# Gates as seven products of half blocks, kept in DRAM until the branch products

## The reference

```
branches = einsum('btgc,gcd->btgd', stack([out_a, out_b, out_c]), w_branch)   # 3 x (512 -> 1024)
gates    = sigmoid(h @ w_gate + b_gate).reshape(b, t, 3, d)                   # 1024 -> 3 x 1024
x        = x + sum(gates * branches, axis=2) @ w_out
h2       = rms_norm(x, norm_ffn)
x        = x + (silu(h2 @ w_ffn_gate) * (h2 @ w_ffn_up)) @ w_ffn_down
```

## Time and profile before

| | us |
|---|---|
| median of 3 runs | 3132.02 |
| lowest and highest | 3129.63, 3132.77 |
| span of the profiled execution, first to last instruction | 3129.0 |

### The profile page before, as it was taken

One profiled execution on the slowest core, in us unless ns is written; L12 is line 12 of the kernel. 1 busy time (PEld: TensorE's weight loads), 2 busy tenths in 40 slices (PEclk: granted clock), 3 DMA queues, 4 the chain that ended last, 5 costly groups with the idle time before them and its releaser, 6 DMA issues.

```text
span 3129.0 us, 50323 instructions
## 1 busy us (share of the span) xinstructions
PE 3066.4 (98%) x18600; PEld 2608.8 (83%) x18600; DVE 1791.4 (57%) x3573; ACT 1329.6 (42%) x2637; POOL 664.3 (21%) x886
## 2 busy tenths in 40 slices
PE   7999999999999999999999999998999999999999
PEld 7988888999999888888788888888977777787777
DVE  6657674353344322345888887876353666753675
ACT  5446565454445221232333333454433555522552
POOL 3423334453542000001111111001101011032240
PEclk9999999999999999999999999999999999999999
DMA  5110011011111321122233225643100000221012
GB/s 204 37 48 18 21 35 51 28 62 44 56 59 46 103 78 51 45 95 97 72 109 109 102 101 204 196 151 140 46 28 22 16 28 15 108 72 67 28 61 101
DMA packets 77412, 231.27 MB, mean 74 GB/s; under 512 B 17712, under 2 KB 21936, under 8 KB 65648
## 3 DMA queue, kind: packets, MB, share of 16 engines
q1 hardware_dynamic: 77168, 228.05, 20.8%
HBM read 183.92 MB, written 43.84 MB: 73 GB/s over the span
## 4 chain that ended last, share of the span: by engine, by line
PE 90%; DVE 6%; ACT 2%; issue 1%; DMA 1%; SPq 0%; POOL 0%; DVEq 0%; ACTq 0%; POOLq 0%
PE ps L2546 71%; PE ps L2589 7%; PE ps L2597 3%; PE ps L2553 2%; PE ps L2604 2%; PE ps L2620 2%; PE ps L2612 1%; PE ps L2623 1%; PE ps L2640 1%; DVE wlo L2815 0%; DVE hlo L2892 0%; ACT hhi L2660 0%; ACT whi L2650 0%; DVE qk L2923 0%; DMA fa2r<-scratch_fs 0%
## 5 line engine op out<-in xcount | busy, mean ns | idle before, releaser
L2546 PE MATMUL ps<-whi,hhi 128*128 128x256 f32 (+2 forms) x1920 | 580.5, 302 | 3.0 <-DVE hlo L2892 1.7
L2546 PE MATMUL ps<-whi,hlo 128*128 128x256 f32 (+2 forms) x1920 | 563.7, 294 | 0.0
L2546 PE MATMUL ps<-wlo,hhi 128*128 128x256 f32 (+2 forms) x1920 | 563.4, 293 | 0.0
L2546 PEld LDWEIGHTS ps<-whi,hhi 128*128 128x128 f32 x1920 | 368.2, 192 | 12.8 <-issue 5.1
L2546 PEld LDWEIGHTS ps<-wlo,hhi 128*128 128x128 f32 x1920 | 368.8, 192 | 7.4 <-issue 0.2
L2546 PEld LDWEIGHTS ps<-whi,hlo 128*128 128x128 f32 x1920 | 368.2, 192 | 7.7
L2546 PE MATMUL ps<-hhi,whi 128*128 128x512 f32 x864 | 342.3, 396 | 0.0
L2546 PE MATMUL ps<-hhi,wlo 128*128 128x512 f32 x864 | 337.0, 390 | 0.0
L2546 PE MATMUL ps<-hlo,whi 128*128 128x512 f32 x864 | 336.3, 389 | 0.0
L3154 POOL TENSOR_SCALAR stats<-stats 128x2 f32<-128x2 f32 (+2 forms) x230 | 59.3, 258 | 1194.1 <-ACT xsf L2654 509.1
L3143 POOL CAST whi<-raw 128x512 fp32r<-128x512 f32 (+4 forms) x180 | 113.7, 631 | 865.8 <-PE ps L2546 856.1
(11 more groups left out here) (616 smaller groups left out, 6996.6 us busy)
## 6 DMA issues: line engine op xcount, KB each, us to landing
raw<-in_W SPq DMA_DIRECT2D x61, 1024.0 KB, 4.8
scratch_fs<-fo SPq DMA_DIRECT2D x77, 256.0 KB, 2.0
raw<-in_W SPq DMA_DIRECT2D x24, 768.0 KB, 4.3
wd<-in_WD SPq DMA_DIRECT2D x44, 256.0 KB, 3.5
wf0b<-in_WF SPq DMA_DIRECT2D x10, 1024.0 KB, 5.3
wf1b<-in_WF SPq DMA_DIRECT2D x10, 1024.0 KB, 5.2
scratch_x<-x SPq DMA_DIRECT2D x16, 512.0 KB, 3.3
orw<-scratch_outs SPq DMA_DIRECT2D x6, 1024.0 KB, 5.8
```

The lines of the kernel that those rows point to most:

```text
L2546: x = e.matmul(r.out, a, b, start=(r.start and m == 0), stop=(r.stop and m == n - 1), skip_group_check=r.joined)
```

## The change

The gates are computed first, for all branches, and stored in a DRAM scratch `gates`; the branch products come after them and read the gates back tile by tile. The 24 strips form 12 pairs (strip x with strip x + 12). The first pair is plain (`plain_gates`: four outputs of 24 matmuls, in eight blocks of 12). For each of the other eleven, the two strips by two halves of tokens and two halves of the 1024 features are a product of 2 by 2 half blocks, made of seven products of 4 k (84 matmuls) whose results are added by VectorE (`ff_add`). For this the token operands t1 to t4 are built from `hhi` and `hlo` (`combine`, `op_split`; t1 in place over the late tokens' first features), on VectorE, partly in attention's tail (`gate_front`), partly among pair 1. Two weight sets alternate. The sums of weights for pair 1 are made by VectorE, for pairs 2 to 11 by GpSimd. The weight stream is now released in three stages (`w_release`), w_branch comes in chunks of 256 columns, and the first and second branch's outputs are split into the space of `hhi` and `hlo`. `b_merge(3, 1)` moves from before the gates into pair 2. `WeightSet`, `combine`, `op_split`, `ff_add` and the product are moved up and shared with the feed-forward, which is otherwise unchanged.

```diff
+GATE_PAIRS = 12
+GATE_STRIPS = [8 * g + d for g in GATE_ORDER for d in range(8)]
...
+    add(("w_gate", 0, 8, [(128 * GATE_STRIPS[x], 128) for x in (0, GATE_PAIRS)]))
+    held = [len(plan)]
     for g in GATE_ORDER:
-        for d in range(8):
-            add(("w_gate", 0, 8, [(g * 1024 + d * 128, 128)]), ("w_branch", g * 512, 4, [(d * 128, 128)]))
+        for c in range(4):
+            add(("w_branch", g * 512, 4, [(256 * c, 256)]))
...
-        def w_release(*free):
-
-            w_held[0] = False
-            raw_free[:], spl_free[:] = [flat(*free), flat(*free)], [flat(*free), flat(*free)]
-            for _ in range(2):
+        def w_release(raws, slots, loads=2):
+            w_stage[0] += 1
+            raw_free[:], spl_free[:] = raws, slots
+            for _ in range(loads):
...
-                    for hf in range(2):
-                        r = Rec()
-                        r.cut = slice(hf * 512, hf * 512 + 512)
-                        r.gate = DB.take()
-                        mm3(r.gate, r.gate.ps[:, :], views(ch.part(0), slice(0, 128)), views(hpair, r.cut), 8, ch.split)
-                        r.si, r.t, r.t_free = scr.take()
-                        r.bias = hb_gate[:, g * 8 + dd:g * 8 + dd + 1]
-                        emit("gate_tanh", r)
-                        gm["gate"] = r.gate.full
-                        halves.append(r)
-                        yield
...
-                            r.branch = DB.take()
-                            gm["branch"] = mm3(r.branch, r.branch.ps[:, :], views(ch.part(1), slice(0, 128)),
-                                               views((ohi, olo), r.cut), 4, ch.split, osp)
-                            r.mix, r.first, r.mix_free = mix[:, dd_, r.cut], first, flat(b_free if dd_ > 3 else b_read) if first else []
-                            r.mixed = r.branch.read if first else signal("mix_added")
-                            emit("gate_mix", r)
...
+            def load(self, i, *free):
+                self.landed = load(self.landing, self.of(i).raw4[:, :, :], self.source[i], *free, self.done[:4])
+            def sums(self, i, *free, pool=False):
+                a11, a12, a21, a22, s1, s2, s4 = self.of(i).raw
+                sum1 = combine(pool, s1, a21, a22, ALU.add, self.landed, self.done[4], *free)
+                sum3 = combine(pool, a21, a11, a21, ALU.subtract)
+                sum2 = combine(pool, s2, s1, a11, ALU.subtract, self.done[5])
+                sum4 = combine(pool, s4, a12, s2, ALU.subtract, self.done[6])
+                self.ready = [self.landed, self.landed, sum3, self.landed, sum1, sum2, sum4]
...
+        g_ops = {
+            "b11": [(lambda k, w=w: w[:, k, early]) for w in hpair], "b21": [(lambda k, w=w: w[:, k + 4, early]) for w in hpair],
+            "b22": [(lambda k, w=w: w[:, k + 4, late]) for w in hpair], "t1": [(lambda k, w=w: w[:, k, late]) for w in (hlo, hhi)],
+            "t2": [(lambda k, w=w: w[:, k, :]) for w in (gt2h, gt2l)], "t3": [(lambda k, w=w: w[:, k, :]) for w in (gt3h, gt3l)],
+            "t4": [(lambda k, w=w: w[:, k, :]) for w in (gt4h, gt4l)],
+        }
...
+        gsets = [
+            WeightSet("wg0", d["WG"], of(0) * 2, of(16) * 2, [of(22, 24, 26, 28, 30, 8, 10)] * 2),
+            WeightSet("wg1", d["WG"], of_rest(80.5) * 2, of(32) * 2, [of(12, 38, 40, 42, 44, 14, 46)] * 2),
+        ]
...
+            gate_kept[x, hf] = store(f"fs{at_ + j}", d["gates"][x, :, 512 * hf:512 * hf + 512], outs[j], r.done)
...
+            def p1(self):
+                self.m1 = self.product(1, self.a.take())
+            def keep(self):
+                evac(self.m1, [(self.x, self.m1.ps[:, :])], gX_free[self.i % 2])
+            def p2(self):
+                self.c11 = self.product(2, self.a.take(), joined=True)
+            def out11(self):
+                gate_out(self.c11.ps[:, :], self.i, 0, self.c11.full, go, go_free, 0, self.c11)
+            def p6(self):
+                self.m6 = self.product(6, self.b.take())
+                ff_add(self.x, self.m6, self.x)
+            def p7(self):
+                self.m7 = self.product(7, self.c.take())
+            def u3(self):
+                ff_add(gU, self.m7, self.x, gU_free)
+            def p5(self):
+                self.m5 = self.product(5, self.d.take())
+            def out22(self):
+                c22 = ff_add(gU, self.m5, gU)
+                gU_free[:] = [gate_out(gU, self.i + GATE_PAIRS, 1, c22, go, go_free, 1)]
+            def p4(self):
+                self.m4 = self.product(4, self.c.take(), joined=True)
+            def out21(self):
+                c21 = ff_add(gV, self.m4, self.x, gV_free)
+                gV_free[:] = [gate_out(gV, self.i + GATE_PAIRS, 0, c21, go, go_free, 2)]
+            def p3(self):
+                self.m3 = self.product(3, self.d.take(), joined=True)
+            def out12(self):
+                c12 = ff_add(self.x, self.m3, self.x)
+                gX_free[self.i % 2] = [gate_out(self.x, self.i, 1, c12, go, go_free, 3)]
...
+        def gate_front():
+            s, b_last = gsets[1], b_vlast[0]
+            s.load(0, b_last, b_fin[2, 3], qk_n_free)
+            yield
+            next(gate_piece)
+            yield
+            gsets[0].load(1, b_last, spl_done[held[0] - 1])
+            yield
+            next(gate_piece)
+            s.sums(0, b_last)
+            yield
+            s.split(0, 0, free=b_last)
+            yield
+            for x, c in enumerate(g_two):
+                near = [b_units[55].v_full, b_units[55].s_full, b_units[55].exps]
+                combine(False, gt3[:, c, :], b_at(g_hi, 1, late, c), b_at(g_hi, 0, late, c), ALU.subtract, near)
+                combine(False, gt3[:, c, :], gt3[:, c, :], b_at(g_lo, 1, late, c), ALU.add)
+                yield
+                next(gate_piece)
+                three[x] = combine(False, gt3[:, c, :], gt3[:, c, :], b_at(g_lo, 0, late, c), ALU.subtract)
+                s.split(0, (2, 1)[x], free=b_last)
+                yield
+            s.split(0, 5, free=b_last)
+            yield
+            for x, c in enumerate(g_two):
+                two[x] = combine(False, gt2[:, c, :], gt3[:, c, :], b_at(g_hi, 0, early, c), ALU.add, b_units[63].s_full)
+            yield
+        gate_gen = gate_front()
...
+                next(gate_gen, None)
...
+        next(gate_piece)
+        s = GatePair(1)
+        near = [b_units[55].s_full, b_units[55].v_full]
+        for x, c in enumerate(g_two):
+            g_read["t3"].append(op_split(gt3[:, c, :], gt3h[:, c, :], gt3l[:, c, :], three[x], two[x], near))
+        for x, c in enumerate(g_two):
+            two[x] = combine(False, gt2[:, c, :], gt2[:, c, :], b_at(g_lo, 0, early, c), ALU.add)
+        four = [combine(False, gt4[:, c, :], b_at(g_hi, 1, early, c), gt2[:, c, :], ALU.subtract, b_read, gp_free) for c in g_two]
+        for x, c in enumerate(g_two):
+            g_read["t2"].append(op_split(gt2[:, c, :], gt2h[:, c, :], gt2l[:, c, :], two[x], four[x], b_read))
+        for _ in range(3):
+            next(gate_piece)
+        drain(gate_piece)
+        s.p1()
+        s.keep()
+        t1_free = [g_plain[0], g_plain[1]]
+        s.p7()
+        for c in g_two:
+            out = gt1[:, c, late]
+            combine(False, out, b_at(g_hi, 0, late, c), b_at(g_hi, 0, early, c), ALU.subtract, t1_free)
+            combine(False, out, out, b_at(g_lo, 0, late, c), ALU.add)
+            one = combine(False, out, out, b_at(g_lo, 0, early, c), ALU.subtract)
+            g_read["t1"].append(op_split(out, hlo[:, c, late], hhi[:, c, late], one, None, None))
+        s.p2()
+        s.out11()
+        s.p6()
+        s.u3()
+        gsets[1].split(0, 4, 3, free=b_vlast[0])
+        s.p5()
+        for x, c in enumerate(g_two):
+            four[x] = combine(False, gt4[:, c, :], gt4[:, c, :], b_at(g_lo, 1, early, c), ALU.add)
+            g_read["t4"].append(op_split(gt4[:, c, :], gt4h[:, c, :], gt4l[:, c, :], four[x], None, b_read))
+        gsets[1].split(0, 6, free=b_vlast[0])
+        s.out22()
+        g_slot = [g_plain[3], b_vlast[0]]
+        gsets[0].sums(1, g_slot, pool=True)
+        gsets[0].split(1, 0, free=g_slot)
+        s.p3()
+        gsets[0].split(1, 5, free=g_slot)
+        s.p4()
+        gsets[0].split(1, 1, 2, free=g_slot)
+        s.out21()
+        s.out12()
+        gsets[1].load(2)
+        gsets[0].split(1, 4, 3, free=g_slot)
...
+        def tile_load():
+            if tiles:
+                x, hf = tiles.pop(0)
+                si, t, free = scr.take()
+                tiles_at.append((si, t, load(f"fa{si}", t[:, :], d["gates"][x, :, sl(512 * hf, 512)], gate_kept[x, hf], free)))
...
+        for i in range(2, GATE_PAIRS):
+            last_m = s.m3.full if i > 2 else s.m4.full
+            s, here, other = GatePair(i), gsets[i % 2], gsets[1 - i % 2]
+            more = i + 1 < GATE_PAIRS
+            if more:
+                other.sums(i, pool=True)
+            else:
```

(79 more changed lines are left out.)

304 lines of the change are left out of this document (165 added, 139 removed).

## The result

| | before | changed |
|---|---|---|
| median, us | 3131.62 (6 runs) | 3141.33 (6 runs) |
| lowest and highest, us | 3129.63, 3132.77 | 3139.56, 3142.3 |
| span of the profiled execution, us | 3129.0 | 3138.9 |
| ratio, 95% interval | | 1.0032 (1.0021 to 1.0042) |

The account below looks back on a forecast made before the run. TensorE bounds the gate stage, busy 380.8 of 380.8 us. Terms -29.9 + 25.2 + 0.7 + 1.6 + 0.7 = -1.7 give a span of 3127.3, plus 3.0 for the median: 3130.3 us, range 3117 to 3142.

Parts of the forecast that it names:

- The saving: Gate stage: 1152 matmuls become 1020, so 132 fewer at 0.2266 us each save 29.9 us, the most possible.
- The last pair: Pair 11: branch weights' split ahead of m1's copy on ScalarE, 7.0 against 5.4 us; +1.6 (0 to 4 with clock drop).
- Loads and splits of the first outputs are in time by 0.5 us: End of pair 11: first branch outputs are loaded and split with 0.5 us to spare, so no loss.
- The entry: Attention's tail and pair 1: VectorE's operand work makes TensorE wait three times; pair 1 ends at 1075.3, not 1050.1: +25.2 us.
- An earlier stall is not to be expected: Attention's tail: no TensorE wait before the last values, as steps are 1.65 us apart and probabilities have two steps' slack.
- Pairs 2 and 3: Only pair 2 loses: weights asked for late behind pair 1's stores, m5's bank free 0.7 us too late; +0.7 us.
- Rival (b): Steady pairs: GpSimd's chain of load, sums, split and add sets the pace; 3141 us at 1.2 us per pair; chance 0.15.
- Rival (a): Entry cheaper: low bound 19.1 us without clock loss gives 3121.9 us, all hidden 3102; chance 0.25.
- Rival (c): Exit dearer: clock falls in pair 11, VectorE's lump not absorbed; +3 to +6, 3133 to 3136 us; 0.10 with (d).
- Rival (d): Entry hits attention earlier: weights landing late hold VectorE before the sums, adding full lateness beyond 1003; chance 0.10 with (c).
- The exit to the row stage: Branch stage: rows of k = 6 and 7 late by 1.6 us where 0.9 was lost before; +0.7, 0 to 4.
- Nothing later changes: After the branch stage: no further gain or loss expected.

Follow-up runs that it names:

- Run 3: Changed kernel with the first branch weights' split queued one product later in pair 11, behind the copy of m1; 3131.0 us, ratio 0.9999.
- run 11: Changed kernel with the split of the second half of branch A's outputs ahead of V's add and tanh in pair 11; 3137.4 us, ratio 1.0019.
- Run 1: Changed kernel with GpSimd's four sums of weights for pair 2 waiting until pair 1's t4 is split; 3136.9 us, ratio 1.0018.
- run 8: Changed kernel with attention's tail's plain matmuls in two lots of 24, at the fifth and tenth step as before the change; 3136.9 us, ratio 1.002.
- run 2: Changed kernel with the load of pair 3's weights on SP ahead of pair 1's last two stores; 3137.7 us, ratio 1.0019.
- run 5: Changed kernel with the sums of weights for pairs 3 to 11 made by VectorE instead of GpSimd; 3140.95 us, ratio 1.0034.
- run 12: On run 9 plus edits of run 8 and run 11: t1 ahead of last plain outputs and copy of m1, b_merge in pair 3; 3113.75 us, 0.9945.
- run 7: Changed kernel with pair 1 plain too, three combinations in attention's tail, pair 2's sums on VectorE, later branch-weight split; 3129.0 us, ratio 0.9992.
- run 9: On run 7, the copy of pair 2's m1 queued on ScalarE ahead of the high halves of t1 and t4; 3131.3 us, ratio 0.9999.
- run 4: Changed kernel with eight combinations for t3 and t2 in attention's tail made by GpSimd instead of VectorE; 3146.5 us, ratio 1.0046.
- run 6: Changed kernel with the edits of Run 1, run 2 and Run 3 together; 3126.6 us, ratio 0.9986.

## Why the prediction was wrong

The forecast was 3130.3 us, a loss of 28.2 us against a saving of 29.9, and so 1.7 us faster than the 3132.0 before. The kernel became 9.7 us slower. The saving was right: the steady pairs take 19.0 us and the branch stage waits for nothing. The losses on the gate stage came to 42.8 us, 14.6 more than forecast: 2.3 at the entry, 2.4 in pairs 2 and 3, 6.4 for the last pair, 4.1 for the first outputs, 0.6 less for the exit. The largest of these, and the one that turned the direction, is the step "The last pair", forecast at +1.6.

- **The last pair: the failing step.** The order was seen (the split stands on ScalarE ahead of the copy of m1), but it cost 5.2 and not 1.6 before product 2, and another 2.8 of low clock behind it: 8.0 in all. It was worked out as a queue of 7.0 us from the pair's start: 2.2 until the load leaves, 3.4 to land, 1.3 for split and copy. In the trace pair 11 begins at 1252.1 (pair 10's product 5 ends at 1246.6, two blocks more), the load leaves at 1256.0 and lands 4.95 later, and the copy starts at 1261.8. The load left 1.8 us later, since the last output of pair 10 stands behind V's tanh, a high half and two splits on ScalarE and VectorE; and 512 KB took 4.95 us, not the 3.4 read between two sizes in the earlier trace rows. They had a store of 256 KB just ahead of them, and the second 512 KB and the 1 MB of outputs were asked for 1.5 and 1.9 us behind them. Then the clock fell: 36 matmuls took 2.8 us more, and the "drop of the clock" stood only in a bound (0 to 4), half of what came. Run 3 takes this one order away and wins 10.3 us, which brings the kernel to the one before; in its trace 7.8 of them lie here. The forecast with this one term as measured, 8.0 instead of 1.6, is 3136.7 us, slower than before by 4.6.
- **"Loads and splits of the first outputs are in time by 0.5 us"** was wrong by 2.7: 2.2 us of waiting, and 1.7 of low clock behind it, both removed in run 11 (4.0 us). The split of half 0 holds V back on VectorE, and half 1's splits stand behind V's tanh.
- **The entry, forecast +25.2, came to +27.5.** VectorE's list was the right mechanism and almost the right length: product 3 started at 1070.2 instead of 1067.7, and the three waits, forecast as 7, 9 and 5 us, were 7.2, 7.0 and 4.2. Inside it two things differed. TensorE's wait in attention's tail was not on the copy of `bPT` but one step earlier, on the bank of a plain gate, whose tanh stood on ScalarE behind the weighting; that weighting waits for VectorE's list, so the time is nearly the forecast one (TensorE goes on at 1026.2; 1026.5 was forecast for the copy). And the first low clock was not hidden: the last values took longer, and t3's high half stands on ScalarE behind their copy, which put VectorE's list 3 us back (its t3 split starts at 1032.7 instead of 1029.7). Against that, contention cost less: the three t1 operations grew by 0.97, 0.97 and 1.11, together 3.1 instead of 3.9, because the third sum ran in VectorE's pause from 1048.4 to 1049.7. Run 1 confirms that they grew by the sums. The exposed clock cost 1.7 instead of 2.2.
- **"An earlier stall is not to be expected"** missed that moving two blocks of 12 ahead of the fifth step delays everything behind them. The 5.4 us were in the sum as a start of 1005.8, but not seen as a price of the change: run 8 undoes the move and wins 4.4.
- **Pairs 2 and 3, forecast +0.7, came to +3.1.** In pair 2 the mechanism and the size were right: the load left at 1080.2 and landed at 1085.4, 8.1 us into the pair, and TensorE waited 0.9 us for m5's bank, though GpSimd's first two sums took 2.02 and 2.10 us beside `b_merge`. Left out was what follows in pair 3: its copy of m1 stands on ScalarE behind the tanh of pair 2's last output, which is late with the splits of the same weights (1.15 and 1.68 us beside the next sums), and TensorE waited another 1.9. In run 2 both waits are gone.
- **Rival (b) did not happen:** run 5 shows the steady pairs indifferent to who makes the sums. That its figure, 3141 us, is the measured one is chance. **Rival (a)** took the opposite view of the entry and fell; its sum also leaves out 1.6 and 0.7 of the forecast's terms and would come to 3124.2 with them. **Rival (c)**, the dearer exit with the clock falling in pair 11, was nearest: from pair 11 to the transposes the loss is 12.2, 9.9 us over the forecast instead of 3 to 6. It shared a chance of 0.10 with (d), and its other half, a lump on VectorE that isn't absorbed, did not come. **Rival (d)** did not happen: the weights for the sums had landed by 1002.1 as forecast, and the sums were done at 1005.2.
- **The exit to the row stage** was misread. The 0.9 us of waits at L3017 in the earlier trace rows lie behind 2700 us, in the second block; between 985 and 1440 us the kernel before waits nowhere. The changed kernel doesn't wait there either, VectorE's lump was absorbed, and the term should have been nothing. "Nothing later changes" holds for the work, but the difference shrank by 2.8 us there, which helped the forecast by chance.

Not settled: those 2.8 us; and why the clock fell behind the wait of 2.2 us in some executions and not in others.

## What to carry to other kernels

When a cheaper product needs prepared operands, the saving is paid in the steady part and the bill comes at the two ends: write out the queue of each in-order engine there, and give the bound engine plain work that needs nothing. A second plain pair costs 2.7 us; with the orders of run 12 it brought pair 3 forward by 16.9 us, but with other orders it gave 2 us over run 3 or none (runs 7 and 9). Put the reader that frees a bank for TensorE ahead of anything that waits for a load, and what the longest list needs ahead of that reader. A wait of a few microseconds on TensorE has to be priced with the slow clock behind it.

## What the runs showed of the hardware

- GpSimd and VectorE hold each other per operation, also when the waiting one is small: 4 columns went from 0.16 to 1.90 us, 512 columns from 0.69 to 2.74 beside GpSimd's operations of 1024 columns (run 4), 1024 columns from 1.24 to 2.21 beside its operations of 512.
- In waits of about 7 us on TensorE the granted clock fell to half; the stretch from 1020 to 1040 us of the changed kernel:

```profile
1020.00:1040.00 20.00, 13.83 (x59) 12.17 (x60) 17.97 (x22) 8.20 (x13) 0.00 (x0) 0.74 0.19 53
```

  that is half speed, 1.2 of 2.4 GHz, for about 10 of the 20 us (0.74 is the mean of 10.4 us at half and the rest at full speed). Behind the wait of 4.9 us in pair 11 the next three blocks of 12 cost 0.93 us more each on average. The Trainium skill (TensorE: Matmul & The Clock Gate, "HAM oscillation — how this bites in real kernels") describes a drop after an idle gap, and these rows agree.
- A wait of 2.2 us on TensorE was followed by half clock in the changed kernel (24 matmuls in 7.1 instead of 5.4 us), and behind the same wait the 732 matmuls took 167.8 us in runs 6 and 9 but 166.2 in runs 3 and 7. No run here shows what decides.
- 512 KB of weights took 4.95 us to land with a store of 256 KB just ahead and loads of 512 KB and 1 MB right behind, about as long as the 5.2 us of a 1 MB load in the earlier trace rows.
